# A second set of down-projection slots and a reordered pass end in a hybrid decoder's expert layer

## The reference, cut to what matters

```python
logits = (tokens @ router_w).astype(jnp.float32)
top_vals, top_idx = lax.top_k(logits, TOP_K)             # TOP_K = 2
top_w = jax.nn.softmax(top_vals, axis=-1)
combine = jnp.sum(jax.nn.one_hot(top_idx, N_EXPERTS, dtype=jnp.float32) * top_w[..., None], axis=1)
out = jnp.zeros_like(tokens)
for e in range(N_EXPERTS):                               # 8
    y = (jax.nn.silu(tokens @ w_gate[e]) * (tokens @ w_up[e])) @ w_down[e]
    out = out + combine[:, e:e + 1].astype(tokens.dtype) * y
```

## Time and profile before

| | |
|---|---|
| runs of the kernel | 2041.2, 2044.34 (median), 2049.78 us |
| profiled execution | 2051.01 us, span 2049.3 us |
| busy share of the span | PE 96%, PEld 85%, DVE 19%, ACT 13%, POOL 4% |
| DMA queue 1 (all data) | 481.55 MB, 62.6% of 16 engines' span |
| mean granted TensorE clock | 0.985 |
| expert weight loads | gate and up x128 each of 896 KB; down x160 of 512 KB and x32 of 1024 KB |

### The profile page before, as it was taken

How to read it: one execution, slowest core, us unless ns; L and a number is a source line. 1 busy time by engine, 2 the same in 40 slices (tenths; PEclk the granted TensorE clock), 3 DMA queues, 4 the chain that set the end, 5 groups by cost and what they waited for, 6 DMA issues and landing times.

```text
span 2049.3 us, 68522 instructions
## 1 busy us (share of the span) xinstructions
PE 1962.7 (96%) x31760; PEld 1736.6 (85%) x31760; DVE 390.6 (19%) x945; ACT 272.5 (13%) x580; POOL 88.3 (4%) x174
## 2 busy tenths in 40 slices
PE   7999999999999999999999799999999999999998
PEld 7888888887778688888888798989899998989897
DVE  3335331110000233632211301010010100000101
ACT  1323223000000122321310000000000000000001
POOL 4011101000000001011100000000000000000000
PEclk9999999999999999999999999999999999999999
DMA  7412123376533142312345689999999999999996
GB/s 240 124 56 91 44 83 116 131 255 204 168 113 103 43 145 63 103 43 63 104 152 200 245 333 414 379 415 376 417 376 417 380 414 415 377 416 378 414 366 254
DMA packets 183535, 483.03 MB, mean 236 GB/s; under 512 B 13118, under 2 KB 111628, under 8 KB 183436
## 3 DMA queue, kind: packets, MB, share of 16 engines
q1 hardware_dynamic: 183436, 481.55, 62.6%
HBM read 480.46 MB, written 1.05 MB: 235 GB/s over the span
## 4 chain that ended last, share of the span: by engine, by line
PE 87%; DMA 7%; DVE 3%; ACT 1%; issue 1%; SPq 0%; POOL 0%; DVEq 0%; ACTq 0%
PE bank L642 36%; PE bank L629 18%; PE bank L1169 7%; DMA pool<-in_moe_w_down_dram 7%; PE bank L734 5%; PE bank L1092 4%; PE bank L1129 4%; PE bank L1108 3%; PE bank L690 2%; PE bank L1296 1%; PE bank L1055 1%; DVE pool L1813 0%; PE bank L1015 0%; PE bank L991 0%; PE bank L870 0%
## 5 line engine op out<-in xcount | busy, mean ns | idle before, releaser
L642 PE MATMUL bank<-pool 128*64 128x80 f32 x21504 | 775.9, 236 | 44.6 <-DMA pool<-in_moe_w_down_dram 36.6
L642 PEld LDWEIGHTS bank<-pool 128*64 128x64 f32 x21504 | 765.9, 139 | 55.9 <-DMA pool<-in_moe_w_down_dram 40.4
L629 PE MATMUL bank<-hnT,pool 128*128 128x256 f32 x1856 | 427.8, 384 | 0.5 <-DVE pool L1875 0.5
L629 PEld LDWEIGHTS bank<-hnT,pool 128*128 128x128 f32 x1856 | 346.2, 190 | 55.2 <-issue 8.8
L2039 DVE TENSOR_TENSOR pool<-pool,bank 128x320 f32<-128x320 f32 x64 | 27.4, 446 | 676.0 <-PE bank L642 676.0
L1169 PEld LDWEIGHTS bank<-hnT,pool 128*128 128x128 f32 x640 | 121.6, 190 | 23.4 <-issue 7.6
L1169 PE MATMUL bank<-hnT,pool 128*128 128x256 f32 x640 | 140.7, 379 | 0.0
L734 PEld LDWEIGHTS bank<-pool 64*64 64x64 f32 x3008 | 94.8, 135 | 17.2 <-issue 11.2
L734 PE MATMUL bank<-pool 64*64 64x32 f32 (+2 forms) x3008 | 103.4, 221 | 2.6 <-DVE pool L1659 1.6
L1584 ACT ACTIVATE pool<-bank 128x320 f32<-128x320 f32 x64 | 25.2, 404 | 544.8 <-PE bank L642 544.8
L1092 PE MATMUL bank<-oT,pool 128*128 128x256 f32 x384 | 85.4, 380 | 0.0
(11 more groups left out here) (318 smaller groups left out, 1170.8 us busy)
## 6 DMA issues: line engine op xcount, KB each, us to landing
pool<-in_moe_w_gate_dram SPq DMA_DIRECT2D x128, 896.0 KB, 13.8
pool<-in_moe_w_up_dram SPq DMA_DIRECT2D x128, 896.0 KB, 11.0
pool<-in_moe_w_down_dram SPq DMA_DIRECT2D x160, 512.0 KB, 10.3
pool<-in_w_in_dram SPq DMA_DIRECT2D x66, 1024.0 KB, 5.4
pool<-in_moe_w_down_dram SPq DMA_DIRECT2D x32, 1024.0 KB, 10.7
pool<-in_ffn_w_gate_dram SPq DMA_DIRECT2D x11, 1024.0 KB, 7.6
pool<-in_ffn_w_up_dram SPq DMA_DIRECT2D x11, 1024.0 KB, 5.5
pool<-in_ffn_w_down_dram SPq DMA_DIRECT2D x11, 1024.0 KB, 5.1
```

The lines of the kernel that those rows point to most:

```text
L629: ins = mm(ps[:, s * T:(s + 1) * T], w[:, k, (j + s) * P:(j + s + 1) * P], hnT[:, k, :], start=(k == 0), stop=(k == KD - 1))
L642: ins = mm(bank[rows, cs], w[:, rows], rhs, start=start, stop=stop, skip_group_check=True)
```

## The change

- A second set of down slots, each set now of three slots of 2, 2 and 3 tiles (1 MB, 1 MB, 1.5 MB). Even down rounds use one set, odd rounds the other. A down load waits for the use of the round two before it.
- SP loads each hidden round in one piece, and the down round behind it; the last two down rounds it issues in a pass are both of the next pass's first half. Down round 1 of the first pass is loaded ahead too, once the output projection of layer 1 is done.
- On TensorE the two down rounds of a half are written out, no longer a loop. `heT` holds 14 tiles, and VectorE no longer waits for the down rounds.
- The selection's weighted copy of a pass (`weighted`) is made in the same pass, and transposed after its down rounds, ahead of the transposes of the outputs; nothing of it is left ahead of the first pass. `gather` is the last thing of a pass and waits for no addition. The hidden matmuls wait for the two parts of the gathered tokens at slots 0 and 4. The scatter's first two products go to B[4] and B[5], where they went to B[0] and B[1].

```diff
--- before.py
+++ after.py
@@ -43,7 +43,7 @@
 PARTS = (range(0, 4), range(4, 7), range(7, 11), range(11, 14))
-DSLOTS = 6
+DSLOTS = 3
 SW = 256
@@ -134,12 +134,16 @@
-        def down_slot(n):
-            lo = KD * HSLOT
-            return pool[:, lo + n * D:lo + (FB if n == DSLOTS - 1 else n + 1) * D].rearrange("p (f n) -> p f n", n=D)
-        assert KD * HSLOT + FB * D <= MRING * SLOT and KD + DSLOTS <= MRING
+        def down_tiles(n):
+            return range(2 * n, FB if n == DSLOTS - 1 else 2 * n + 2)
+        def down_slot(r, n):
+            lo, tiles = KD * HSLOT + r * FB * D, down_tiles(n)
+            return pool[:, lo + tiles[0] * D:lo + (tiles[-1] + 1) * D].rearrange("p (f n) -> p f n", n=D)
+        assert KD * HSLOT + 2 * FB * D <= MRING * SLOT and KD + 2 * DSLOTS <= MRING
@@ -223,7 +227,7 @@
         xgT = region(KD * CAP).rearrange("p (k n) -> p k n", k=KD)
-        heT = region(FB * CAP).rearrange("p (j n) -> p j n", j=FB)
+        heT = region(HT * CAP).rearrange("p (j n) -> p j n", j=HT)
         yT = region(KD * CAP).rearrange("p (k n) -> p k n", k=KD)
@@ -251,7 +255,7 @@
         slot_loaded = [sem(f"slot{i}_loaded") for i in range(MRING)]
-        hid_loaded, dwn_loaded = slot_loaded[0:KD], slot_loaded[KD:KD + DSLOTS]
+        hid_loaded, dwn_loaded = slot_loaded[0:KD], (slot_loaded[KD:KD + DSLOTS], slot_loaded[KD + DSLOTS:KD + 2 * DSLOTS])
         hid_used = sem("hidden_used")
@@ -468,6 +472,7 @@
+        sums = lambda half, t: (B[4], B[5], proj[0], proj[1])[2 * half + t]
         norm_bank = lambda t, q: (B[4], B[5], B[0], B[1])[2 * t + q]
@@ -1225,20 +1230,16 @@
                 for t in range(NT):
-                    ins = pe.transpose(B[2][0:CAP, t * P:(t + 1) * P], selw[:, t, :], ident[:])
+                    ins = pe.transpose(B[0][0:CAP, t * P:(t + 1) * P], selw[:, t, :], ident[:])
                 ins.then_inc(selT_mm, 1)
...
                 gather(0)
-                pe.wait_ge(xg_ready, 1)
-                selection_rows(0)
                 pe.wait_ge(passes_ready, 1)
...
                 with pe.Fori(0, n_pass) as i:
-                    pe.wait_ge(xg_ready, i * 2 + 2)
-                    pe.wait_ge(selT_ready, i + 1)
                     pe.wait_ge(sc_added, i * 4 + 4)
@@ -1248,6 +1249,8 @@
                             for n in range(KD):
+                                if n % 4 == 0:
+                                    pe.wait_ge(xg_ready, i * 2 + (n // 4 + 1))
                                 pe.wait_ge(hid_loaded[n], i * (32 * NH) + h * 32 + side * 16 + 16 * (slot_count[n] + 1))
@@ -1264,40 +1267,39 @@
-                            for f in range(FB):
-                                if f == PARTS[0][0] or f == PARTS[1][0]:
-                                    pe.wait_ge(hid_free, i * (8 * NH) + h * 8 + r * 2
-                                               + (ff_base + 8 + (1 if f == PARTS[0][0] else 2)))
-                                n, at = min(f, DSLOTS - 1), max(f - (DSLOTS - 1), 0)
-                                if at == 0:
-                                    pe.wait_ge(dwn_loaded[n], i * (16 * NR) + h * 32 + r * 16 + 16 * (slot_count[KD + n] + 1))
-                                for k in range(KD):
-                                    ins = columns_mm(B[4 + k // 4], slice(k % 4 * CAP, (k % 4 + 1) * CAP),
-                                                     down_slot(n)[:, at, k * P:(k + 1) * P], heT[:, f, :],
-                                                     start=False, stop=False)
-                                    if f == FB - 1 and k % 4 == 3:
-                                        ins.then_inc(dwn_mm, 1)
+                            for n in range(DSLOTS):
+                                pe.wait_ge(dwn_loaded[r][n], i * (16 * NH) + h * 16
+                                           + 16 * (slot_count[KD + DSLOTS * r + n] + 1))
+                                for f in down_tiles(n):
+                                    if f == PARTS[0][0] or f == PARTS[1][0]:
+                                        pe.wait_ge(hid_free, i * (8 * NH) + h * 8
+                                                   + (ff_base + 8 + 2 * r + (1 if f == PARTS[0][0] else 2)))
+                                    for k in range(KD):
+                                        ins = columns_mm(B[4 + k // 4], slice(k % 4 * CAP, (k % 4 + 1) * CAP),
+                                                         down_slot(r, n)[:, f - down_tiles(n)[0], k * P:(k + 1) * P],
+                                                         heT[:, FB * r + f, :], start=False, stop=False)
+                                        if f == FB - 1 and k % 4 == 3:
+                                            ins.then_inc(dwn_mm, 1)
                                 if n < DSLOTS - 1:
...
                             hidden(side)
-                        with pe.Fori(0, 2) as r:
+                        for r in range(2):
                             down(r)
+                    selection_rows(i)
                     for half in range(2):
...
                         ins.then_inc(ye_mm, 1)
+                    pe.wait_ge(selT_ready, i + 1)
                     for half in range(2):
+                        pe.wait_ge(ye_ready, i * 2 + (half + 1))
                         for t in range(NT):
-                            if half or t == 0:
-                                pe.wait_ge(ye_ready, i * 2 + (max(half, t) + 1))
-                            ins = mm((B[0], B[1], proj[0], proj[1])[t + 2 * half][:, :], selwT[0:CAP, t * P:(t + 1) * P],
+                            ins = mm(sums(half, t)[:, :], selwT[0:CAP, t * P:(t + 1) * P],
                                      ye[0:CAP, half * 512:half * 512 + 512], start=True, stop=True)
                             ins.then_inc(sc_mm, 1)
-                    selection_rows(i + 1)
-                    pe.wait_ge(sc_added, i * 4 + 6)
                     gather(i + 1)
@@ -1983,10 +1985,11 @@
-            def places(i):
-                place = lambda k, t: rs[:, 16 + 2 * k + t:17 + 2 * k + t]
-                share = lambda k, t: rs[:, 12 + 2 * k + t:13 + 2 * k + t]
+            place = lambda k, t: rs[:, 16 + 2 * k + t:17 + 2 * k + t]
+            share = lambda k, t: rs[:, 12 + 2 * k + t:13 + 2 * k + t]
+            def selected(i):
                 for t in range(NT):
@@ -1994,6 +1997,9 @@
                 ins.then_inc(sel_ready, 1)
+            def weighted(i):
                 for t in range(NT):
@@ -2002,7 +2008,6 @@
                 ins.then_inc(selw_ready, 1)
                 v.wait_ge(selw_ready, i + (selw_base + 1))
@@ -2016,39 +2021,36 @@
                 v.wait_ge(selT_mm, i + 1)
-                v.tensor_copy(selwT[0:CAP, :], B[2][0:CAP, 0:T]).then_inc(selT_ready, 1)
+                v.tensor_copy(selwT[0:CAP, :], B[0][0:CAP, 0:T]).then_inc(selT_ready, 1)
...
                 v.memset(rs[:, 62:63], 0.0).then_inc(hid_free, 4)
-                places(0)
+                selected(0)
                 pass_table()
...
                 gathered(0)
-                selection_rows(0)
                 def one_pass(i, last):
...
                         for q in range(4):
-                            lo, n, g = PARTS[q][0], len(PARTS[q]), q % 2
+                            lo, n = PARTS[q][0], len(PARTS[q])
                             v.wait_ge(hid_mm, i * (8 * NH) + (hid_base + 8 * h + 4 + q + 1))
-                            if q == 2:
-                                v.wait_ge(dwn_used, i * ((DSLOTS - 1) * NR) + ((DSLOTS - 1) * 2 * h + 4))
-                            if q == 3:
-                                v.wait_ge(dwn_mm, i * (2 * NR) + (down_base + 4 * h + 2))
-                            tt(heT[:, PARTS[g][0]:PARTS[g][0] + n, :], sge[:, lo:lo + n, :],
+                            tt(heT[:, lo:lo + n, :], sge[:, lo:lo + n, :],
                                (B[2], B[3], proj[0], proj[1])[q][:, 0:n * CAP].rearrange("p (f n) -> p f n", f=n),
...
                         if h == 0:
-                            places(i + 1)
+                            weighted(i)
+                            selected(i + 1)
+                    selection_rows(i)
                     for half in range(2):
...
                             cs = slice(half * 512, half * 512 + 512)
-                            ins = tt(x[:, t, cs], x[:, t, cs], (B[0], B[1], proj[0], proj[1])[t + 2 * half][:, :], ALU.add)
+                            ins = tt(x[:, t, cs], x[:, t, cs], sums(half, t)[:, :], ALU.add)
                             ins.then_inc(all_added if last and half else sc_added, 1)
                     if not last:
-                        selection_rows(i + 1)
                         gathered(i + 1)
@@ -2136,9 +2138,9 @@
-                lo, hi = (r * FB + n) * P, (r * FB + (FB if n == DSLOTS - 1 else n + 1)) * P
+                lo, hi = (r * FB + down_tiles(n)[0]) * P, (r * FB + down_tiles(n)[-1] + 1) * P
```

(20 more changed lines are left out.)

## The result

The changed kernel takes 2082.77 us, median of 4 runs (2077.84 to 2088.7), against 2047.06 us for the kernel before beside it (4 runs, 2041.2 to 2052.22): ratio 1.0177, 95% interval 1.0133 to 1.022. It is slower; the forecast was 1996 and its range ended at 2025.

What follows compares the result with a forecast made beforehand. Transfers were taken to bound each pass, afterwards 105.5 us against TensorE's 103.1. First issue 1155.2 + stream 755.8 + idle 8.3 + 2.1 + 65.2 + 5.2 + 8.7 gave a 2000.5 us span, forecast as 1996; range 1984 to 2025.

Steps and rivals of the forecast that it cites:

- zero either way: TensorE's steady-state cost of writing out both down rounds: the removed 0.2 us branch left no gap, so nothing gained or lost.
- The section on the rule: Warned that TensorE's pass of about 2010 instructions might not loop in a 2048-instruction store without fetching; price about 2020 us.
- no stall in 75 fetches before 1140: Evidence that TensorE's straight code has its next 16 KB piece fetched ahead, used against refetching stalls.
- Rival 1: Code fetched again at a pass's two long backward jumps, 2.7 us each; 108.5 us a pass, 2024 us; chance 0.18.
- Rival 3: Code fetched on demand throughout, 16 pieces a pass at 2.7 us; 2325 us, slower from the third stall; chance 0.06.
- The dry stretch of the queue in pass 0: Weights' queue empties once, before half 1's up round: 6.3 us by slots plus 2 for restart, 8.3 us idle.
- the up round of half 0: Sign of being right: TensorE's waits move here from the down loads, 0.2 us each and a longer first.
- the 103.1: TensorE's own need per pass in us after the change, down from 104.4; between 102.6 and 104.4.
- the code of pass 0: New code may stall TensorE in pass 0: 2.7 us as already seen, plus 0 to 2.7 more, taken as 0.
- slot 7 of the last pass's first up round: The last load that can be late; the stream up to it is 315.6 MB, 755.8 us at 417.6 GB/s.
- The new end: Selection transposed at its pass's end, gather last: TensorE 104.4 to 103.1 us a pass, and 1.0 us before pass 0.
- refetching in every form 0.24: Chances given to code being fetched again: 0.18 at the two long backward jumps, 0.06 on demand all the time.

## Why the prediction was wrong

**The step that failed: both down rounds written out, "zero either way" in steady state.** It priced the taken branch that goes away and not the body that grows. Measured, the 448 instructions more cost 2082.77 - 2006.45 = 76 us in this kernel and 89 in the kernel before. In pass 2 the sum is: 12.0 us of TensorE's idle time against 2.8 with the hint (118.77 - 106.79; 105.62 - 102.80), and 106.79 against 102.80 us of busy time, 4.0 us more for the same records, which the slow clock after the gaps makes longer. 9.2 + 4.0 is the 13.2 us between the two passes.

**The section on the rule named the danger, its number (about 2010; counted 1989) and the store of 2048, and then gave it too little.** What spoke against it was "no stall in 75 fetches before 1140". That row stood for straight code under 43 to 255 GB/s of other traffic. Pass 0 of the same trace had the other case, 2.70 us at 1169.47 under full traffic, and it was used as a price of one event and not as a sign that every fetched piece would now be late. By the Trainium skill, "Runtime: NRT & Kernel Launch", section "Instruction fetch mechanics", TensorE's store has 2048 instructions in blocks of 256: the runs agree as far as eight pieces stay with the hint and seven without. The same section of the Trainium skill has a window of two blocks outside which a branch stalls. The runs contradict it: 1541, 1733 and 1791 instructions loop without one packet. The Trainium skill also says there that the cost of crossing a block is mostly hidden. That holds in the steady passes at 51 GB/s of traffic, not at 372 to 380, where four crossings of a pass cost 0.6 to 2.2 us each.

**Rival 1** had the jumps, but at 2.7 us each and both of them: measured one of 5.5, none at the half. (The section on the rule prices this rival at about 2020, the rival itself at 2024; both are faster than the kernel before, and the measured time is not.) **Rival 3** had the right kind, refetching through the pass, and a wrong size: 9 packets and five gaps of 2.2 us in the mean, not 16 of 2.7. It had the right threshold, though: from about 8 us of stalls a pass is slower than before, and 11.2 is past it.

**The other steps** can be read in the kernel with the hint, which is the forecast's kernel in all but the code. Its span is 2005.5 against 2000.5, its median 2006.5 against 1996.

The dry stretch of the queue in pass 0, at its place and size (5 us steps; last column GB/s):

```profile
1200.00:1205.00 5.00, 4.18 (x121) 4.02 (x119) 0.00 (x0) 0.00 (x0) 0.00 (x0) 1.00 0.61 243
1205.00:1210.00 5.00, 4.82 (x138) 4.66 (x136) 0.00 (x0) 0.00 (x0) 0.00 (x0) 1.00 0.18 26
1210.00:1215.00 5.00, 5.00 (x150) 5.00 (x148) 0.00 (x0) 0.00 (x0) 0.00 (x0) 1.00 1.03 358
1215.00:1220.00 5.00, 5.00 (x152) 5.00 (x149) 0.00 (x0) 0.00 (x0) 0.00 (x0) 1.00 0.91 351
```

Four steps at 417.6 would be 1670; these sum to 978, so 692 x 5 / 417.6 = 8.3 us are lost: the forecast's 8.3. That it agrees to the tenth is partly luck, since 2.0 of the 8.3 were picked out of a range from 0 to 5. The first issue was at 1154.86 (forecast 1155.2). Steady passes took 105.6 to 105.8 at 417 GB/s (105.5 at 417.6), and TensorE's waits are at the up round of half 0, where they were to be. In 1365 to 1893 us:

```profile
PE bank L647 <- DMA pool<-in_moe_w_up_dram: 9.0, 5, 1.9
```

TensorE's busy time of 102.8 a pass bears out the 103.1, and so does pass 0, whose 108.72 us less the five gaps below are 103.4. Right in direction and short in size: the code of pass 0, where five gaps sum to 5.3 us (0.62, 1.63, 0.61, 1.64, 0.82) and 2.7 + 0 was taken; two of them:

```profile
1167.71 24.73 PE L647 MATMUL bank<-pool 128*64 128x80 f32 x701 [1.63 <-issue]
...
1199.34 4.64 PE L647 MATMUL bank<-pool 128*64 128x80 f32 x127 [1.64 <-issue]
```

The stream's first 45 us, 1154.86 to 1200, ran at 383 GB/s, which is 3.7 us short of 417.6, where the sum had 1.1. With the rate of 417 (315.6 MB: 1.1 us more) that is 3.7 of the 5.0 us by which the span was missed. The whole miss lies ahead of slot 7 of the last pass's first up round, which TensorE began at 1926.68 where the sum has 1155.2 + 755.8 + 8.3 + 2.1 = 1921.4; the rest of it I can't place. The new end, forecast at 1.3 us of TensorE's time a pass and 1.0 at the start, gave 6 us by itself. I take it that with one set of slots part of what TensorE saves is passed on, since the queue waits for TensorE; no run shows this apart.

The range failed for one reason: the forecast held a store that 1541 instructions were known to fit, a body of 2010, a size of 2048, and gave refetching in every form 0.24, most of it at a price at which the kernel still won. A bound from both sides, as at the other steps, would have had the 2.7 us of the earlier trace rows at every piece on one side.

## What to carry to other kernels

Count the instructions of a loop before its code is unrolled, in pieces of 16 KB and with the place where it starts: here, without the hint, a loop over seven pieces never fetched again, one over eight did in every pass, and a shift of 64 instructions cost 139 us. Where the loop must be that large, a prefetch hint on its backward branch kept all eight pieces for 31 ns a pass and turned 1.8% slower into 1.9% faster; why it does is not shown. Idle time that ends in "issue" together with packets on the instruction queue is the sign to look for, and code that ran without a gap under light traffic says nothing of what a fetch costs under full traffic.

## What was not expected of the hardware

- The loop's backward branch, where the pass's code does not stay, takes 6.1 us on TensorE's sequencer while the weights stream at about 400 GB/s; TensorE stands 5.5 us (4.1 to 5.7 over the four kernels that fetch under this traffic). At 51 GB/s it stands 2.8 to 3.2 us.
- A gap of 5.5 us leaves TensorE at a granted clock of 0.50 for the 5 us after it: 62 records in place of 143.
- The branch hint's reach is wider than the jump: the four gaps within the pass went with it.
- A record of an f32 matmul of 128 weight columns with 80 moving ones took 115 ns, two records of 64 columns 35 each.
